# Attention scores and value products in plain fp32 in place of split fp32r, with two buffers for turned probabilities

## The reference

```python
def _mha(q, k, v):
    s = jnp.einsum('bhqd,bhkd->bhqk', q, k).astype(jnp.float32) * HEAD_DIM ** -0.5
    p = jax.nn.softmax(s, axis=-1).astype(v.dtype)
    return jnp.einsum('bhqk,bhkd->bhqd', p, v)
```

## Time and profile before

| | |
|---|---|
| median of 3 timed runs | 2691.57 us (2691.43 to 2697.0) |
| profiled execution | 2693.0 us, its span 2691.0 us |
| TensorE busy | 92% of the span, 13056 products |
| VectorE, ScalarE busy | 64%, 40% |
| mean granted TensorE clock | 0.968 of 2.4 GHz |

### The profile page before, as it was taken

One profiled execution on the slowest core, in us unless ns is written; L12 is line 12 of the kernel. 1 busy time (PEld: TensorE's weight loads), 2 busy tenths in 40 slices (PEclk: granted clock), 3 DMA queues, 4 the chain that ended last, 5 costly groups with the idle time before them and its releaser, 6 DMA issues.

```text
span 2691.0 us, 32893 instructions
## 1 busy us (share of the span) xinstructions
PE 2486.0 (92%) x13056; PEld 2074.2 (77%) x13056; DVE 1711.7 (64%) x2812; ACT 1073.7 (40%) x1854; POOL 29.3 (1%) x47
## 2 busy tenths in 40 slices
PE   6999998999999997889999989999988988878998
PEld 3788786777777775767887868887877878767998
DVE  3888686465566566679887873333357566677554
ACT  4222235355444434362222352223345545445344
POOL 0000000000000000000000000000000000000000
PEclk8999999999999999999999999999999999989999
DMA  5655553222212121126555533232333333223555
GB/s 220 224 198 188 171 184 130 86 67 91 75 52 71 53 73 55 55 86 208 191 191 169 188 94 102 94 97 87 103 114 115 112 102 110 79 80 109 173 173 156
DMA packets 98073, 331.47 MB, mean 123 GB/s; under 512 B 11009, under 2 KB 12033, under 8 KB 97281
## 3 DMA queue, kind: packets, MB, share of 16 engines
q1 hardware_dynamic: 97922, 329.39, 36.5%
HBM read 323.06 MB, written 6.29 MB: 122 GB/s over the span
## 4 chain that ended last, share of the span: by engine, by line
PE 76%; DVE 13%; ACT 6%; issue 3%; DMA 1%; SPq 0%; POOL 0%; DVEq 0%; ACTq 0%
PE ps L318 22%; PE ps L309 22%; PE ps L310 22%; PE ps L1123 4%; PE ps L1097 2%; DVE stat L1422 2%; DVE w_low L298 2%; PE ps L1107 1%; PE ps L622 1%; ACT prob L1245 1%; DVE pt_low L1464 1%; ACT w_high L292 1%; DVE tmp L604 1%; DMA raw<-in_weights 1%; DVE h L573 1%
## 5 line engine op out<-in xcount | busy, mean ns | idle before, releaser
L298 DVE TENSOR_TENSOR w_low<-raw,w_high 128x1024 fp32r<-128x1024 f32 (+1 forms) x488 | 553.1, 1136 | 507.0 <-ACT w_high L292 506.1
L309 PE MATMUL ps<-u_high,w_high 128*128 128x512 f32 (+1 forms) x2304 | 820.2, 367 | 12.8 <-DVE hid_low L701 10.9
L310 PE MATMUL ps<-u_low,w_high 128*128 128x512 f32 (+1 forms) x2304 | 810.6, 363 | 0.0
L292 ACT ACTIVATE w_high<-raw 128x1024 fp32r<-128x1024 f32 (+1 forms) x488 | 481.9, 990 | 807.2 <-DMA raw<-in_weights 806.1
L318 PE MATMUL ps<-u_high,w_low 128*128 128x512 f32 (+1 forms) x2496 | 547.6, 363 | 5.8 <-DVE w_low L298 5.8
L309 PEld LDWEIGHTS ps<-u_high,w_high 128*128 128x128 f32 x2304 | 446.6, 194 | 92.2 <-DVE hid_low L701 12.3
L310 PEld LDWEIGHTS ps<-u_low,w_high 128*128 128x128 f32 x2304 | 446.6, 194 | 62.9
L318 PEld LDWEIGHTS ps<-u_high,w_low 128*128 128x128 f32 x2496 | 425.7, 191 | 82.4 <-DVE w_low L298 7.1
L381 DVE CUSTOM_DVE_ANT_0 ps<-mod_raw,c_all,smalls 128x1024 f32<-128x1024 f32 x256 | 319.3, 1289 | 0.3 <-DMA mod_raw<-in_mods 0.2
L309 PE MATMUL ps<-hid_high,w_high 128*128 128x512 f32 (+1 forms) x704 | 252.2, 367 | 8.8 <-DVE hid_low L701 8.8
L310 PE MATMUL ps<-hid_low,w_high 128*128 128x512 f32 (+1 forms) x704 | 251.7, 366 | 0.0
(11 more groups left out here) (163 smaller groups left out, 2621.7 us busy)
## 6 DMA issues: line engine op xcount, KB each, us to landing
raw<-in_weights SPq DMA_DIRECT2D x360, 512.0 KB, 3.5
mod_raw<-in_mods SPq DMA_DIRECT2D x128, 512.0 KB, 4.3
raw<-in_weights SPq DMA_DIRECT2D x64, 384.0 KB, 3.0
raw<-in_weights SPq DMA_DIRECT2D x64, 320.0 KB, 2.8
mod_first<-in_mods SPq DMA_DIRECT2D x16, 512.0 KB, 13.4
h_kept<-h SPq DMA_DIRECT2D x16, 256.0 KB, 2.0
na_bias<-in_na_rows SPq DMA_DIRECT2D x16, 256.0 KB, 3.8
h<-h_kept SPq DMA_DIRECT2D x2, 2048.0 KB, 8.6
```

The costliest lines, as they stand in the source:

```text
L292: act.activation(w_high[:, s, 0:width], raw[s][:, 0:width], ACT.Copy).then_inc(high_made.sem, 1)
L298: dve.tensor_tensor(w_low[s][:, 0:width], raw[s][:, 0:width], w_high[:, s, 0:width], ALU.subtract).then_inc(low_made.sem, 1)
L309: pe.matmul(o, w_high[:, s, w], x_high(x), start=first and a == 0, stop=False)
L310: pe.matmul(o, w_high[:, s, w], x_low(x), start=False, stop=False)
```

## The change

Queries, keys, values and turned probabilities are no longer split. One fp32 tile each takes the place of a high and a low one; ScalarE's copies stay, VectorE's subtractions for them go, and TensorE makes one fp32 product in place of three fp32r ones. The turned probabilities get two buffers, one for even and one for odd pairs, and ScalarE's wait for the value product is one pair later. The results of the branches (q_high, q_low), the weights and the normed input stay split, and the modulation tiles stay on VectorE.

```diff
-        k_high = place("k_high", [BT, S_ALL], F32R, at_mix + 16 * KB)
-        k_low = place("k_low", [BT, S_ALL], F32R, at_mix + 24 * KB)
-        v_high = place("v_high", [4, BW], F32R, at_mix + 32 * KB)
-        v_low = place("v_low", [4, BW], F32R, at_mix + 40 * KB)
+        q_all = place("q_all", [BT, S_ALL], F32, at_mix)
+        k_all = place("k_all", [BT, S_ALL], F32, at_mix + 16 * KB)
+        v_all = place("v_all", [4, BW], F32, at_mix + 32 * KB)
...
-        pt_high = place("pt_high", [2, 4, 2 * P], F32R, at_mix + 48 * KB)
-        pt_low = place("pt_low", [2, 4, 2 * P], F32R, at_mix + 56 * KB)
+        pt = place("pt", [2, 2, 4, 2 * P], F32, at_mix + 48 * KB)
...
-                pe.wait_ge(self.part_low.sem, self.part_low.at(len(self.prep)))
-                pe.wait_ge(self.v_low.sem, self.v_low.at(4))
+                pe.wait_ge(self.part_made.sem, self.part_made.at(len(self.prep)))
+                pe.wait_ge(self.v_made.sem, self.v_made.at(4))
...
-                    for a, (qq, kk) in enumerate(((q_high, k_high), (q_high, k_low), (q_low, k_high))):
-                        for s in range(2):
-                            rows = slice(s * HD, (s + 1) * HD)
-                            m = pe.matmul(ps[:, s, 0:nkeys], qq[rows, t, q:q + P], kk[rows, kt, key:key + nkeys], start=a == 0, stop=a == 2)
+                    for s in range(2):
+                        rows = slice(s * HD, (s + 1) * HD)
+                        m = pe.matmul(ps[:, s, 0:nkeys], q_all[rows, t, q:q + P], k_all[rows, kt, key:key + nkeys], start=True, stop=True)
...
-                        pe.wait_ge(self.pt_low.sem, self.pt_low.at(j))
+                        pe.wait_ge(self.pt_made.sem, self.pt_made.at(j))
...
-                    pe.wait_ge(self.pt_low.sem, self.pt_low.at(2 * p + 2))
+                    pe.wait_ge(self.pt_made.sem, self.pt_made.at(2 * p + 2))
...
-                    heads = [(s, c, vv, pp) for s in range(1 if b == "A" else 2) for c in range(nkeys // P)
-                             for vv, pp in ((v_high, pt_high), (v_high, pt_low), (v_low, pt_high))]
+                    heads = [(s, c) for s in range(1 if b == "A" else 2) for c in range(nkeys // P)]
...
-                        m = pe.matmul(into, vv[:, key // P + c, col * P:(col + 1) * P], pp[:, s, c], start=a % n == 0, stop=a % n == n - 1)
+                        m = pe.matmul(into, v_all[:, key // P + c, col * P:(col + 1) * P], pt[:, p % 2, s, c], start=a % n == 0, stop=a % n == n - 1)
...
-                    if j >= 2:
-                        act.wait_ge(self.mixed.sem, self.mixed.at(j // 2))
-                    act.activation(pt_high[:, 0:ns, 0:nkeys // P, half], ps[:, 2:2 + ns, 0:nkeys].rearrange("p s (c q) -> p s c q", q=P),
-                                   ACT.Copy).then_inc(self.pt_high.sem, 1)
+                    if j >= 4:
+                        act.wait_ge(self.mixed.sem, self.mixed.at(j // 2 - 1))
+                    act.activation(pt[:, j // 2 % 2, 0:ns, 0:nkeys // P, half], ps[:, 2:2 + ns, 0:nkeys].rearrange("p s (c q) -> p s c q", q=P),
+                                   ACT.Copy).then_inc(self.pt_made.sem, 1)
...
-                    low_of_probs(j)
...
-                    for v in (v_high, v_low):
-                        pool.memset(v[:, :, HD:HD + P].bitcast(F32), 0.0).then_inc(self.v_zeroed.sem, 1)
+                    pool.memset(v_all[:, :, HD:HD + P], 0.0).then_inc(self.v_zeroed.sem, 1)
```

More of the change, by code:

```diff
@@ L885, in __init__ @@
                 self.roped, self.normed = b != "B", b == "C"
-                self.prep = [(BT + i, S_ALL, k_high[:, i], k_low[:, i]) for i in range(self.nk)]
-                self.prep += [(i, T, q_high[:, i], q_low[:, i]) for i in range(BT)]
+                self.prep = [(BT + i, S_ALL, k_all[:, i]) for i in range(self.nk)]
+                self.prep += [(i, T, q_all[:, i]) for i in range(BT)]
                 n = len(self.prep)
@@ L933, in __init__ @@
                 self.v_turned = signals.new("v_turned", 4)
-                self.v_zeroed = signals.new("v_zeroed", 2 if b == "C" else 0)
-                self.v_high = signals.new("v_high_made", 4)
-                self.v_low = signals.new("v_low_made", 4)
+                self.v_zeroed = signals.new("v_zeroed", 1 if b == "C" else 0)
+                self.v_made = signals.new("v_made", 4)
                 self.head_squared = signals.new("head_squared", n if self.normed else 0)
@@ L954, in __init__ @@
                 self.flipped = signals.new("probs_turned", J)
-                self.pt_high = signals.new("probs_high_made", J)
-                self.pt_low = signals.new("probs_low_made", J)
+                self.pt_made = signals.new("turned_probs_made", J)
                 self.mixed = signals.new("values_mixed", NP)
@@ L1075, in tensor @@
                         if i < 4:
-                            pe.wait_ge(self.v_low.sem, self.v_low.at(i + 1))
+                            pe.wait_ge(self.v_made.sem, self.v_made.at(i + 1))
                         else:
@@ L1112, in mix @@
                     vt = t if self.nk == BT else 0
-                    pe.wait_ge(self.pt_low.sem, self.pt_low.at(2 * p + 2))
+                    pe.wait_ge(self.pt_made.sem, self.pt_made.at(2 * p + 2))
                     if p >= 2:
                         pe.wait_ge(self.o_done.sem, self.o_done.at(p - 1))
-                    heads = [(s, c, vv, pp) for s in range(1 if b == "A" else 2) for c in range(nkeys // P)
-                             for vv, pp in ((v_high, pt_high), (v_high, pt_low), (v_low, pt_high))]
+                    heads = [(s, c) for s in range(1 if b == "A" else 2) for c in range(nkeys // P)]
                     apart = b == "B"
                     n = len(heads) // 2 if apart else len(heads)
-                    for a, (s, c, vv, pp) in enumerate(heads):
+                    for a, (s, c) in enumerate(heads):
                         into = ps[:, 4 + p % 2, s * S_X:(s + 1) * S_X] if apart else ps[:, 4 + p % 2, 0:S_X]
                         col = s if self.padded else vt
-                        m = pe.matmul(into, vv[:, key // P + c, col * P:(col + 1) * P], pp[:, s, c], start=a % n == 0, stop=a % n == n - 1)
+                        m = pe.matmul(into, v_all[:, key // P + c, col * P:(col + 1) * P], pt[:, p % 2, s, c], start=a % n == 0, stop=a % n == n - 1)
                     m.then_inc(self.mixed.sem, 1)
@@ L1190, in head_square @@
             def head_square(self, act, i):
-                slot, W, _, _ = self.prep[i]
+                slot, W, _ = self.prep[i]
                 if past(i - 1):
@@ L1194, in head_square, with keep_qk @@
                 act.activation(sq[:, i % 2, 0:W], proj[:, slot, 0:W], ACT.Square).then_inc(self.head_squared.sem, 1)
-            def high_of_qk(self, act, i):
-                slot, W, hi, lo = self.prep[i]
+            def keep_qk(self, act, i):
+                slot, W, into = self.prep[i]
                 if self.roped:
                     act.wait_ge(self.turned.sem, self.turned.at(i + 1))
-                act.activation(hi[:, 0:W], proj[:, slot, 0:W], ACT.Copy).then_inc(self.part_high.sem, 1)
+                act.activation(into[:, 0:W], proj[:, slot, 0:W], ACT.Copy).then_inc(self.part_made.sem, 1)
             def scalar(self, act):
@@ L1215, in scalar @@
                     act.wait_ge(self.v_turned.sem, self.v_turned.at(tt + 1))
-                    into, of = self.values(v_high, tt)
-                    act.activation(into, of, ACT.Copy).then_inc(self.v_high.sem, 1)
+                    into, of = self.values(v_all, tt)
+                    act.activation(into, of, ACT.Copy).then_inc(self.v_made.sem, 1)
                 for i in self.head_items(0):
@@ L1233, in scalar @@
                     for i in items:
-                        self.high_of_qk(act, i)
+                        self.keep_qk(act, i)
                 def exps(j):
@@ L1247, in exps, with keep_probs @@
                     e.then_inc(self.expd.sem, 1)
-                def high_of_probs(j):
+                def keep_probs(j):
                     nkeys, ns = self.steps[j][3], 1 if b == "A" else 2
@@ L1298, in scalar @@
                     self.window_results(act, 1 + 2 * j)
-                    high_of_probs(j)
+                    keep_probs(j)
                     if j % 2 == 0 and j:
@@ L1382, in vector @@
                 dve.wait_ge(self.staged.sem, self.staged.at(self.staged_at))
[L1383 to L1387, removed]
+                for kind, c, turn, _ in self.carriers():
                     if kind == "mix":
@@ L1400, in vector @@
                     self.ropes(dve, turn)
-                    for i in items:
-                        self.low_of_qk(dve, i)
                 def row_max(j):
@@ L1458, in scale_probs @@
                         m.then_inc(self.probs.sem, 1)
[L1460 to L1465, removed]
                 def low_of_out(p):
@@ L1528, in pool @@
```

(7 more changed lines are left out.)

11 lines of the change are left out of this document (3 added, 8 removed).

## The result

The changed kernel takes 2663.92 us (median of 4 runs, 2661.94 to 2666.68) against 2691.50 before on the same chip: ratio 0.9896, 95% interval 0.9877 to 0.9914, a gain of about 28 us. The forecast was 2674 with 2648 to 2713, and faster. Run once more beside a later experiment, it gave 2665.38 us, ratio 0.9898 (0.9882 to 0.9915).

The account below looks back on a forecast made before the run. TensorE, 92% busy, was taken as the bound, its passes traded against waits for VectorE's subtractions. 13.5 + 19.0 - 21 - 4 - 8.7 - 4 - 4 - 8 = -17.2 us gave 2674 us, range 2648 to 2713.

Parts of the forecast that it names:

- Scores: Score steps on TensorE: fp32 in place of three fp32r products, two heads side by side, costs +13.5 us.
- the first rival: Score steps: heads don't overlap in fp32; 2709 us with three instruction times (chance 0.11), 2743 with four (0.06).
- Value products: Value products on TensorE: 560 fp32 instructions in place of 840 fp32r products cost +19.0 us.
- Waits before value products: TensorE's waits for low halves of turned probabilities, 25.5 us: only ScalarE's copy is then needed, -21 us.
- Before turns: TensorE's turns in layer 0 waited 5.1 us for the low half of the step before; -4 us.
- First scores: First score of each of eight branches, waiting 20.4 us for low halves of queries and keys; -8.7 us.
- Weight low halves: Layer 1: TensorE's 5.8 us of waits for weights' low halves behind VectorE's queue; -4 us.
- Waits before scores: TensorE's 31.5 us of waits on exponentials, both layers: row maximum and exponentials stay, so only -4 us.
- the second rival: Mixers: waits move to the exponentials; 2711 us in full (chance 0.05), about 2693 at half (0.11).
- Clock: Softmax stretches: 53 us at 1.2 GHz, much of it idle; fewer long stalls give -8 us.

Follow-up runs that it names:

- same_rows: The changed kernel with both heads of a score step read from partitions 0 to 63, sharing the array's rows; 2730.83 us, ratio 1.0144.

## Why the prediction was right, and where its size was off

- **Scores**: forecast +13.5 us. The step of 512 keys went from 1057.58 - 1056.68 = 0.90 us before to 561.45 - 560.39 = 1.06 after, the step of 256 keys from 0.55 to 0.63: 64 x 0.16 + 32 x 0.08 = +12.8 (the short steps are 1101.60 to 1102.15 before, and 1093.55 to 1094.18 after). Right; the overlap, taken from the modulation units, was shown by same_rows, and the first rival fell.
- **Value products**: forecast +19.0 us. 560 x 0.216 - 840 x 0.120 = +20.2. Right; both prices taken, 0.124 us before and 0.22 us after, were a little high, which evens out.
- **Waits before value products**: forecast -21, measured 25.5 - 4.3 = -21.2, with ScalarE's copy named as the new releaser. **Before turns**: forecast -4 of layer 0's 5.1, measured 7.4 - 1.4 = -6.0 over both layers, with another 7.0 - 5.9 = -1.1 on scaled probabilities, which the forecast left out. **First scores**: forecast -8.7, measured 20.4 - 11.8 = -8.6; D of layer 1 gained 3.8 as worked out. **Weight low halves**: forecast -4, measured 5.8 - 4.8 = -1.0.
- **Waits before scores**: forecast -4, measured 31.5 - 30.7 = -0.8. They didn't grow, so the second rival fell. That VectorE reaches the row maximum earlier by as much as TensorE reaches the score is how I read it; no run tests it.
- **Clock**: forecast -8, and this is the term that was mis-sized. The passes cost 12.8 + 20.2 = 33.0 us by the two lines above, and TensorE's busy time rose by 12.4 only: 21 us of busy time went elsewhere. Instruction by instruction the trace has TensorE busy for 128 us at 1.2 GHz before and 83 after; half of the difference, 22.5 us, is the same loss read directly. I had taken much of the time at the lower level for idle. In the step stretches it is not: 71 of 75 us of it were busy before (and 30 of 31 after). The level can be down when work has come back after a pause. Behind the 3.03 us stall of the earlier trace rows, in 4.60 us, TensorE is busy for 4.56 and the granted clock is 0.50 (columns as in the earlier trace rows):

```profile
1091.40:1096.00 4.60, 4.56 (x21) 4.56 (x22) 2.82 (x9) 1.54 (x5) 0.00 (x0) 0.50 0.01 4
```

There the pause and the slow work behind it are both paid. The profiled run of before stood at 0.968, lower than the median 0.972 of its later runs; by the runs' clocks (0.978 to 0.982 after) the time at 1.2 GHz fell by 42 us, which is 21 us of loss if TensorE was busy in it.

The sum with measured terms, the clock's read directly: 12.8 + 20.2 - 38.6 - 22.5 = -28.1, against the spans' difference of -26.2. So the forecast's direction rests on the mechanism it named and not on luck. Its size fell short by 10 us, as the clock gave 14 us more than forecast, while the idle terms together gave 38.6 us in place of 41.7. They came that near partly by luck: weights and scores' waits gave 6 us less than forecast, and turns 3 us more. What stays open is how the clock's gain is shared: the end of the waits alone brings the time at 1.2 GHz from 151 to 124 us, the passes alone to 137, both to 109. The levels add up, but no run here held the clock with the rest unchanged, so that the 21 to 22 us are the clock's is read from traces and not tested by itself.

## What to carry to other kernels

Ask of a split product not only what its passes cost but who makes the low half and behind what that stands in its queue: here fp32 was 33 us dearer on an engine 92% busy, and still won 28 us. Price a stall twice where the product behind it starts at 1.2 GHz: the pause, and the same work at half speed. And look for the layout that lets two half-height products run side by side before counting each head's fp32 product for itself; it decided the sign. When a wait is to be moved out of a queue, first see in the trace at which steps it arises: here most of it arose ahead of the loop that was reordered.

## What the runs showed of the hardware

- An fp32 product is two instructions, each 0.216 us for 256 columns; fp32r costs 0.120 us for 256 columns in a row of 24. So at 256 columns an fp32 product costs 3.6 fp32r products, and at 512 columns, by the earlier trace rows, 0.86 / 0.23 = 3.7.
- Two heads on rows 0 to 63 and 64 to 127 overlap in fp32 too. The four weight loads of a step are over in 0.30 us, as the row below shows, and the step measured 1.06 us: two instruction times of 0.43 and some 0.20 for its start. In same_rows it measured 543.91 - 542.00 = 1.91 us, four of them and the same start. The four instructions start at 0, 0.007, 0.534 and 0.540 us, and in same_rows at 0, 0.533, 0.962 and 1.391 us. The Trainium skill ("TensorE: Matmul & The Clock Gate", Part 3: Packing small matmuls) has matmuls start strictly in order. Read with the two instructions of a call next to each other, that would have given three instruction times, 1.29 us and the start. The step shows two, so either the order in the queue alternates between the heads or the rule doesn't bind across row groups. The trace can't tell which.

```profile
560.39 0.30 PEld L1091 LDWEIGHTS ps<-k_all,q_all 64*128 64x128 f32 x4 [0.35 <-issue]
```
